# One-pass sample state updates in a retention layer, with the gate's sample sum and the first loads moved

## What is computed

```python
def retention_chunk(state, q, k, v, log_g):
    ...
    inner = jnp.einsum('bhts,bshe->bthe', scores, v)
    cross = jnp.einsum('bthd,bhde->bthe', q * q_decay[None, :, :, None], state)
    k_decay = jnp.exp((t - 1.0 - i)[:, None] * log_g[None, :])
    new_state = jnp.exp(t * log_g)[None, :, None, None] * state + jnp.einsum('bshd,bshe->bhde', k * k_decay[None, :, :, None], v)
    return new_state, inner + cross

def ret_output(x, o, g, w_out):
    on = standardize(o).reshape(bsz, t, R_V_WIDTH)
    return x + (jax.nn.silu(g.astype(F32)) * on).astype(x.dtype) @ w_out
```

## Time and profile before

| | |
|---|---|
| median of 3 runs | 3490.93 us (3487.97 to 3492.68) |
| the profiled execution | 3490.97 us, span 3489.2 us |
| mean granted TensorE clock | 0.979 |
| busy: TensorE, VectorE, ScalarE, GpSimd | 94%, 26%, 29%, 30% of the span |
| DMA | 107 GB/s over the span |
| instructions | 41826 |

### The profile page before, as it was taken

One profiled execution on the slowest core, in us unless ns is written; L12 is line 12 of the kernel. 1 busy time (PEld: TensorE's weight loads), 2 busy tenths in 40 slices (PEclk: granted clock), 3 DMA queues, 4 the chain that ended last, 5 costly groups with the idle time before them and its releaser, 6 DMA issues.

```text
span 3489.2 us, 41826 instructions
## 1 busy us (share of the span) xinstructions
PE 3290.9 (94%) x15122; PEld 2567.9 (74%) x15122; DVE 916.1 (26%) x1684; ACT 998.0 (29%) x1526; POOL 1052.2 (30%) x444
## 2 busy tenths in 40 slices
PE   7999999999997999999999999999999989999976
PEld 5887777777886786776768677676867768878865
DVE  2202343332033413222130322214132240120335
ACT  5523333233233421312212131221212221222332
POOL 5632322332331232322313222231322223333311
PEclk9999999999999999999999999999999999999998
DMA  6432222223232243333333333333333344322332
GB/s 241 142 85 89 62 68 61 73 66 119 79 103 81 96 148 121 119 103 102 110 116 118 118 117 100 104 110 121 114 119 106 125 140 140 119 92 79 103 98 84
DMA packets 211053, 374.22 MB, mean 107 GB/s; under 512 B 20449, under 2 KB 59329, under 8 KB 207617
## 3 DMA queue, kind: packets, MB, share of 16 engines
q1 hardware_dynamic: 137744, 233.34, 21.5%
q10 hardware_dynamic: 73152, 138.60, 11.8%
HBM read 312.71 MB, written 60.16 MB: 107 GB/s over the span
## 4 chain that ended last, share of the span: by engine, by line
PE 75%; DVE 5%; ACT 2%; issue 1%; DVEq 1%; DMA 1%; ACTq 0%
PE bank L606 18%; PE bank L608 17%; PE bank L607 17%; PE bank L610 5%; PE bank L611 4%; PE bank L622 3%; PE bank L1032 2%; PE bank L1023 2%; PE bank L1071 1%; PE bank L1067 1%; PE bank L1063 1%; DVE R L1994 1%; DVEq L1782 1%; DVE R L2235 1%; PE bank L928 1%
## 5 line engine op out<-in xcount | busy, mean ns | idle before, releaser
L583 POOL TENSOR_TENSOR w_lo<-w_raw,w_hi 128x1024 fp32r<-128x1024 f32 x440 | 1052.0, 2391 | 2391.7 <-ACT w_hi L1138 2391.2
L606 PE MATMUL bank<-w_hi,xT_hi 128*128 128x512 f32 (+1 forms) x2880 | 1172.9, 407 | 6.5 <-ACT R L1150 2.7
L608 PE MATMUL bank<-w_hi,xT_lo 128*128 128x512 f32 (+1 forms) x2880 | 1125.2, 391 | 0.0
L607 PE MATMUL bank<-w_lo,xT_hi 128*128 128x512 f32 (+1 forms) x2880 | 1123.5, 390 | 0.0
L1138 ACT ACTIVATE w_hi<-w_raw 128x1024 fp32r<-128x1024 f32 x440 | 466.2, 1059 | 1537.6 <-PE bank L611 1437.8
L606 PEld LDWEIGHTS bank<-w_hi,xT_hi 128*128 128x128 f32 x2880 | 546.2, 190 | 144.3 <-issue 34.1
L608 PEld LDWEIGHTS bank<-w_hi,xT_lo 128*128 128x128 f32 x2880 | 544.6, 189 | 116.2
L607 PEld LDWEIGHTS bank<-w_lo,xT_hi 128*128 128x128 f32 x2880 | 546.0, 190 | 114.1 <-issue 11.5
L610 PE MATMUL bank<-w_hi,xT_sample 128*128 128x512 f32 (+1 forms) x816 | 333.4, 409 | 59.8 <-DVE R L1868 59.1
L611 PE MATMUL bank<-w_lo,xT_sample 128*128 128x512 f32 (+1 forms) x816 | 320.8, 394 | 0.0
L622 PE MATMUL bank<-cst,R 128*128 128x128 f32 (+3 forms) x1274 | 192.9, 277 | 61.5 <-DMA R<-in_norm_mem 13.5
(11 more groups left out here) (180 smaller groups left out, 2095.2 us busy)
## 6 DMA issues: line engine op xcount, KB each, us to landing
w_raw<-in_w_in_ret SPq DMA_DIRECT2D x128, 512.0 KB, 3.7
w_raw<-in_w_in_even SPq DMA_DIRECT2D x80, 512.0 KB, 3.6
w_raw<-in_w_in_ret SPq DMA_DIRECT2D x128, 256.0 KB, 2.9
R<-in_state_ret ACTq DMA_DIRECT2D x64, 512.0 KB, 4.4
out_ret_state_sample<-R ACTq DMA_DIRECT2D x64, 512.0 KB, 3.0
w_raw<-in_w_out_ret SPq DMA_DIRECT2D x64, 512.0 KB, 3.7
w_raw<-in_w_out_even SPq DMA_DIRECT2D x32, 512.0 KB, 3.7
mix_scratch<-R ACTq DMA_DIRECT2D x16, 576.0 KB, 3.4
```

The lines of the kernel that those rows point to most:

```text
L583: pool.tensor_tensor(wlo[:, s], raw[:, s], whi[:, s].bitcast(F32), ALU.subtract).then_inc(lo_ready, 1)
L606: pe.matmul(acc, th[:, k, tok], hi[:, kk, 0:width], start=first, stop=False)
L607: pe.matmul(acc, th[:, k, tok], lo[:, kk, 0:width], start=False, stop=False)
L608: mm = pe.matmul(acc, tl[:, k, tok], hi[:, kk, 0:width], start=False, stop=last)
```

## The change

Keys and values of the samples are laid out as four copies of 32 tokens (four sequences each, `g` says which four): keys high, low, high, low against values high, high, low, low. One matmul with 128 rows then sums all four products of a sequence. `spread_keys` makes the key copies of a head, scaled by the decay, once a head; `batch_keys` only masks them for a sequence. `spread_values` makes the values; its signal `vx_ready` is now given for each half. The gate's sample sum goes ahead of the wait for the square root (`group_vars` is split off `group_norm`). At the start the memory's gains come first and in one load, the other gains in two loads behind the memory rows with a transpose at the end of the first memory chunk, the conversions of the first weight groups alternate with the first scaled copies, and x is loaded in the first memory chunk.

```diff
-                    if b == 0 and m == 0:
-                        pe.wait_ge(vx_ready, h + 1)
-                    for part in range(2):
-                        mm = pe.matmul(bk[:, :], kzb[:, b % 2, part * RK + m * P:part * RK + (m + 1) * P], Vx,
-                                       start=(part == 0), stop=(part == 1))
+                    if b < 2 and m == 0:
+                        pe.wait_ge(vx_ready, 2 * h + (b + 1))
+                    mm = pe.matmul(bk[:, :], kzb[:, b % 2, m * P:(m + 1) * P], Vx[:, ORD[b] // 4], start=True, stop=True)
...
             act.dma_start(cst[:, :], consts).then_inc(consts_in, 16)
+            act.dma_start(grow, I.norm_mem.rearrange("l (k p) -> (l k) p", p=P)).then_inc(gains_in, 16)
             for m in range(2):
                 act.dma_start(memX[:, m], I.mem_prompt[0, m * P:(m + 1) * P, :]).then_inc(mem_in, 16)
...
-            load_x(False)
-            for s in range(RING):
-                hi(Lin(0), s)
+            for n, g in enumerate((I.norm_mix, I.norm_cross)):
+                act.dma_start(xgrow[GM * n:GM * (n + 1), :], g.rearrange("l (k p) -> (l k) p", p=P)).then_inc(xgains_in, 16)
+            hi(Lin(0), 0)
             act.wait_ge(*is_full("mem", "gains"))
...
             for n in range(3):
                 hi_half("mem", n, n, 0, "norm_mem0")
+                hi(Lin(0), n + 1)
...
+                    if g == 2:
+                        load_x(False)
...
-            def double_keys():
-                v.tensor_copy(QK[NS:2 * NS, NT, RK:2 * RK], QK[0:NS, NT, RK:2 * RK])
+            def spread_keys(h):
+
+                for g in range(2):
+                    keys = QK[HB * g:HB * (g + 1), NT, RK:2 * RK]
+                    for q in range(2):
+                        v.tensor_scalar(kr[HB * q:HB * (q + 1), g], keys, 1.0, None, ALU.mult)
                 v.drain()
+                do(v.tensor_scalar(kr[NS:2 * NS], kr[0:NS], 1.0, None, ALU.mult))
+                do(v.tensor_scalar(kr, kr, C("kq")[:, bass.ds(h, 1)], None, ALU.mult))
+                do(v.tensor_scalar(kzb, kr, 1.0, None, ALU.mult))
+                do(v.scalar_tensor_tensor(kq, kzb.bitcast(F32), klow, kr, ALU.mult, ALU.add))
+
+            def spread_values(h):
+
+                for g in range(2):
+                    rows_of = V[HB * g:HB * (g + 1), NT]
+                    for q in range(2):
+                        v.tensor_scalar(Vx[HB * q:HB * (q + 1), g], rows_of, 1.0, None, ALU.mult)
+                    v.drain()
+                    for q in range(2):
+                        ins = v.scalar_tensor_tensor(Vx[NS + HB * q:NS + HB * (q + 1), g], Vx[HB * q:HB * (q + 1), g].bitcast(F32), -1.0,
+                                                     rows_of, ALU.mult, ALU.add)
+                    do(ins.then_inc(vx_ready, 1))
...
             def batch_keys(h, b):
-                keys, col = QK[:, NT, RK:2 * RK], kz[:, bass.ds(DEC_B * h + ORD[b], 1)]
-                do(v.tensor_scalar(kzb[:, b % 2, 0:RK], keys, col, None, ALU.mult))
-                do(v.scalar_tensor_tensor(kzb[:, b % 2, RK:2 * RK], keys, col, kzb[:, b % 2, 0:RK].bitcast(F32), ALU.mult, ALU.subtract)
-                   .then_inc(kz_ready, 1))
+                n = ORD[b]
+                do(v.tensor_scalar(kzb[:, b % 2], kq[:, n // 4], kmask[:, n % 4:n % 4 + 1], None, ALU.mult).then_inc(kz_ready, 1))
...
                 group_stats(NT)
+                group_vars(h)
+                v.wait_ge(w_used, Lin(L.c + GPC, L.k, L.i).at(GPC))
+                sample_sum(sgs[0:NS, :], bank[NT], FREE(stage, ("C", NT)))
                 group_norm(h)
-                gate_mul(stage, "C", i, 2 + h, Lin(L.c + GPC, L.k, L.i), lambda t: ON[0:rows(t), t], sg, sgs, NT)
-
-            double_keys()
+                gate_mul(stage, "C", i, 2 + h, None, lambda t: ON[0:rows(t), t], sg, sgs, NT)
```

More of the change, by code:

```diff
@@ L91, in shape_constants @@
     put("kd", g[None] ** (P - 1 - i[:, None]) * RK ** -0.5)
-    kz = np.zeros((NS, RH, DEC_B))
-    kz[s, :, s // DEC_T] = g[None] ** (DEC_T - 1 - s[:, None] % DEC_T) * RK ** -0.5
-    put("kz", np.concatenate([kz.reshape(NS, -1)] * 2))
+    put("kq", g[None] ** (DEC_T - 1 - row_t[:, None]) * RK ** -0.5)
+    put("kmask", (i[:, None] % HB) // DEC_T == np.arange(DEC_B // 2)[None])
+    put("klow", -((i // HB) % 2.0))
     put("gp", np.tile(np.concatenate([g ** P, g ** DEC_T]), (P, 1)))
@@ L147 @@
 GORD = [4, 5, 0, 1, 2, 3, 6, 7]
-GAINS = ["norm_mix0", "norm_mix1", "norm_cross0", "norm_cross1", "norm_mem0", "norm_mem1"]
+GAINS = ["norm_mem0", "norm_mem1", "norm_mix0", "norm_mix1", "norm_cross0", "norm_cross1"]
+GM = 2 * KT
+GX = 4 * KT
 EARLY = {8: 0, 13: 1, 18: 2, 23: 3, 28: 4}
@@ L232, in make_plan @@
     weights("mem", 4)
-    plan.add("mem", [("gains", 5, True)])
+    plan.add("mem", [("gains", 5, True), ("xgains", 4, True)])
     state.xt = 1
@@ L418, in build @@
         qz, zm, rdec = c.take(2, DEC_B, HB), c.take(DEC_B, NS), c.take(P + NS)
-        kzb = split[:, 0:4 * RK].rearrange("p (s n) -> p s n", s=2)
-        Vx = split[:, 4 * RK:]
+        kr, kq = c.take(2, RK), c.take(2, RK)
+        kzb = split[:, 0:2 * RK].rearrange("p (s n) -> p s n", s=2)
+        Vx = split[:, 2 * RK:].rearrange("p (g n) -> p g n", g=2)
         raw_loaded = [sem(f"raw_loaded{s}") for s in range(RING)]
@@ L681, in _ @@
             pe.wait_ge(consts_in, 16)
-            pe.wait_ge(gains_in, 16 * len(GAINS))
+            pe.wait_ge(gains_in, 16)
             pe.wait_ge(*is_free("mem", "gains"))
-            tp(bank_of("mem", "gains")[:, 0:KT * len(GAINS)], grow[0:KT * len(GAINS), :], KT * len(GAINS)).then_inc(FULL("mem", "gains"), 1)
+            tp(bank_of("mem", "gains")[:, 0:GM], grow, GM).then_inc(FULL("mem", "gains"), 1)
             pe.wait_ge(mem_in, 32)
@@ L697, in mem_step @@
                     xt_half("mem", g + 3, memX, g + 3)
+                elif ch == 0 and g == GPC - 1:
+                    pe.wait_ge(xgains_in, 32)
+                    pe.wait_ge(*is_free("mem", "xgains"))
+                    tp(bank_of("mem", "xgains")[:, 0:GX], xgrow, GX).then_inc(FULL("mem", "xgains"), 1)
                 elif ch == 1:
@@ L1292, in mem_his @@
                 elif ch == 1:
+                    if g == 0:
+                        act.wait_ge(*is_full("mem", "xgains"))
+                        copy(gT[:, GM:GM + GX], bank_of("mem", "xgains")[:, 0:GX]).then_inc(FREE("mem", "xgains"), 1)
+                        act.drain()
                     hi_half("mem", GPC + g, g, 256, "norm_mem1")
@@ L1996, in gate_mul @@
                     between()
-                v.wait_ge(w_used, L.at(GPC))
-                sample_sum(sbuf[0:NS, :], bank[NT], FREE(stage, (tag, NT)))
+                if L is not None:
+                    v.wait_ge(w_used, L.at(GPC))
+                    sample_sum(sbuf[0:NS, :], bank[NT], FREE(stage, (tag, NT)))
                 v.wait_ge(sil_ready, n + 1)
@@ L2228, in group_norm @@
                 do(v.tensor_scalar(stat[0:NS, 55:56], stat[0:NS, 73:74], qd2[0:NS, sam], EPS, ALU.mult, ALU.add).then_inc(var_ready, 1))
+            def group_norm(h):
+                own, sam = bass.ds(h, 1), bass.ds(h + RH, 1)
                 v.wait_ge(std_ready, plan.st["gn"] + 1 + h)
```

23 lines of the change are left out of this document (10 added, 13 removed).

## The result

The changed kernel takes 3409.8 us (median of 4 runs, 3408.18 to 3411.18); the kernel before, beside it, 3491.35 us. The ratio is 0.9768, with a 95% interval of 0.9751 to 0.9785: faster by 2.3%, where the forecast was 3.0%, and 1.8 us above the top of the range. The profiled execution took 3408.18 us (span 3406.4), so 82.8 us of span are gone where 105.1 were forecast.

The account below looks back on a forecast made before the run. TensorE, busy nine tenths or more of nearly every slice, was taken as the bound; states 29.4, gate sums 60.7, last head 5 and first loads 10 made 105.1 us off 3490.97, so 3386 us, range 3377 to 3408.

Parts of the forecast that it names:

- the first loads: Start of the kernel: first weight matmul at 14.9 us instead of 24.49, worth 10 us, bounds 5 to 11.
- Nothing is late, but I keep 3 us for it: First loads: weight groups beside x take 5 to 6 us, TensorE needs one in 3.3; 3 us kept in the bounds.
- The gate's sample sum: End of seven heads' gate chunks: sum ahead of norm removes an 8.67 us stall each, 60.7 us, at least 46.7.
- rival (1): Gated transposes wait behind gate products held up by a split: 2 us in seven heads, 3400 us; chance 0.12.
- The last head: Sum ahead of the last head's norm: 5 us gained, bounds 2 and 7, some 4 us waiting at the transposes.
- The states: Sample states in one pass: 128 fewer matmuls at 0.23 us, 29.4 us, if nothing new waits.
- The term for the split: State copies held up by GpSimd's weight split: 0 taken, 4 us over 8 heads kept as the other end.
- (2): VectorE sets the states' pace; TensorE waits for banks as long as the removed matmuls took: 3415 us; chance 0.05.
- (3): State copies cost 2.1 us each by themselves, making the second state 5 us late in 8 heads: 3426 us; chance 0.04.
- (4): Each of eight state copies and subtractions waits for a whole split of 2.37 us: 3501 us, slower; chance 0.02.
- (5): Sample tile waits on another account, so only the rest, 44 us, is gained: 3447 us; chance 0.02.
- The third: Sign of being wrong, at the first loads: TensorE waits for weights while x loads.

Follow-up runs that it names:

- kernel with x two groups apart: Changed kernel plus splits held back, earlier memory root, three last-head mix splits moved, and x's five loads two groups apart from chunk 0's group 4: 3377.51 us, ratio 0.9666.
- kernel with held splits: Changed kernel plus one ScalarE wait per head, so the next weight rounding comes only after the four gate products: 3394.04 us, ratio 0.9714.

## Why the prediction was wrong

**The step that failed is the first loads.** The prediction gave them 10 us, bounds 5 to 11. In this pair of profiles they cost 5.3 us up to the spatial transposes (265.48 to 270.82), so 15.3 of the 22.3 us that are missing lie here. Of the rest, 3.5 lie in the six periods (11.76 us less in place of 16 x 0.23 + 8.67 = 12.35) and 3.5 behind head 6's sample statistics (13.9 us less in place of 17.4). The size varies from execution to execution, but no profile with these loads as they stand shows a gain of more than 4.4 us. The first half of the step was right within its bounds: the first weight matmul came at 16.42 against 14.9 forecast. What failed is "Nothing is late, but I keep 3 us for it". The pace was not the error: a group of weights beside x was priced at 5 to 6 us, and the mean was 5.5. But I set the four groups in hand against TensorE's need for weights. TensorE never ran out of weights. It waited for ScalarE, which works three to four groups ahead of TensorE in one fixed order, so that the root and the evacuation of chunk 0 stand behind roundings of chunk 1's weights. For that work the groups in hand were no cover at all. And the weights did not come at their mean pace: ScalarE got one group at 38.49 and the next at 48.94, with the root behind it. The kernel with x two groups apart shows the same step giving 9 to 12 us.

**The gate's sample sum: right in mechanism, too large by a little.** 7.75 us a head alone, where 8.67 were priced. The difference, 0.9 us, is about the new wait of 1.00 us, and that is the norm's. I named GpSimd's splits as the claimant of 2.8 us of slack, and weighed them against the gate products alone, at 1.5 us for two. They hit the norm ahead of these: two of its five instructions are held up, and it takes 6.88 us where the kernel with held splits takes 3.05. So rival (1) came true at half its price: 1.00 us a head in place of 2. I had the row that warned of it, the cast of 2.11 us, and applied it to instructions that read two SBUF operands and to copies, not to the norm.

**The last head**: 5 us forecast, with some 4 us of waiting at the transposes; 8.43 came, for the same reason: one split holds up the 128x4 step ahead of the norm, another the norm. The held splits take it back to 4.37, about the forecast's figure. Of the 13.9 us behind head 6's statistics one period is 11.8, so the last head gave some 2 us, the low bound.

**The states: right.** 27 us alone against 29.4; no wait at the first two states. The term for the split was put at nothing, and the hold-up did come: one copy of a head's four. That it cost nothing is in part luck, as a copy costs 0.42 us by itself against 0.61 priced, and the second state was on time by 0.1 us. Rivals (2), (3) and (4) did not happen; nor did (5).

**The signs of being wrong.** Two of the three came. The eight copies and subtractions took 6.4 us (1329.47 to 1335.88) where 6 was the sign, and nothing waited for them. The second gate product ended 12.9 us after the chunk's start where 12 was the sign, and the transposes waited. The third did not come: TensorE waited while x loaded, but for a bank that ScalarE had to empty, and the sign looked for weights.

The bounds show what was wrong with the range: only the first loads left theirs. I bounded each new wait at its place, but the burst of x had its price bounded at 3 us by a cover that I had not traced through ScalarE's order.

## What to carry to other kernels

When a load is moved, follow every engine that handles what it delays in that engine's own order, and look for what else stands behind; buffers in hand on the last engine of a chain do not cover an earlier one that runs ahead. Here a burst of large rows on one queue took most of the bytes from another queue of small rows, so issue such a burst in pieces at the pace of the work beside it, and look at when each load is whole, not at the mean pace. When a wait goes, ask what the engine that waited will now start early and on whom it falls: here one wait put back on ScalarE was worth 1.07 us a head. A step of two columns counts as much as one of 512 where it meets such work on the path that others wait for.

## What the runs showed of the hardware

- A VectorE tensor_scalar is held up by GpSimd's split like a cast: 547 ns at the median and 2466 at the most for 128x512, 2.41 us against 0.23 for 128x4, and 2.15 to 2.37 against 0.17 for 128x2, where a scalar_tensor_tensor is held up too (2.27 us). Without a split beside it none of 40 in the norm took over 550 ns. The Trainium skill (SBUF — State Buffer, "SBUF: two separate sides") speaks of a lock for a whole instruction; the tensor_scalar that ends at 1420.44, 0.28 us after the split, agrees.
- Two DMA queues with work shared by packets, not by bytes: 271 and 267 packets, 1.97 and 0.51 MB, in the 6 us from 34 to 40.
- A load can land long after its queue has moved as many bytes: one of 0.52 MB took 20.5 us, while its queue moved 1.89 MB in 20 us.
- The same program's wait at chunk 1 was 7.45, 10.75 and 15.00 us in three executions (the first with the held splits, whose first 60 us are the same work).
